# Sparse attention in head pairs with a turned value product, and key selection by counting bits over six row blocks at once

## The reference

```python
sc = jnp.where(pos[None, None, :] <= tb[None, :, None], sc, NEG)
_, idx = lax.top_k(sc, topk)              # topk = 256
dist = tb[None, :, None] - idx
o_a = sparse_attend(qa_blk, take_rows(k_a, idx), take_rows(v_a, idx), dist >= 0, dist, table_a)
...
s = jnp.einsum('bqgrd,bqkgd->bqgrk', qg, k_sel).astype(f32) * HEAD_DIM ** -0.5
s = jnp.where(valid[:, :, None, None, :], s + bias, NEG)
p = jax.nn.softmax(s, axis=-1).astype(v_sel.dtype)
o = jnp.einsum('bqgrk,bqkgd->bqgrd', p, v_sel)
```

## Time and profile before

| | us |
|---|---|
| three runs | 3072.55, 3091.87, 3098.43; median 3091.87 |
| the profiled execution | 3101.05, its span 3099.2 |
| mean granted clock of PE | 0.925 of 2.4 GHz |
| projection, first half with the indexer's scores | 0 to 236 |
| projection, second half | 236 to 517.8 |
| window attention | 517.8 to 643 |
| sparse attention, blocks 0 and 1 | 643 to 690 |
| sparse attention, blocks 2 and 3 | 690 to 757 |
| sparse attention, blocks 4 and 5 (to 852.8) | from 757 |
| sparse attention, blocks 6 and 7 | to 930 |
| sample attention | 930 to 1018 |
| merge | 1018 to 1077 |
| output projection, MLPs, recurrent mixer | 1077 to 3099 |

### The profile page before, as it was taken

How to read it: one execution, slowest core, us unless ns; L and a number is a source line. 1 busy time by engine, 2 the same in 40 slices (tenths; PEclk the granted TensorE clock), 3 DMA queues, 4 the chain that set the end, 5 groups by cost and what they waited for, 6 DMA issues and landing times. The chain is left out here.

```text
span 3099.2 us, 39640 instructions
## 1 busy us (share of the span) xinstructions
PE 2863.1 (92%) x15920; PEld 2603.2 (84%) x15920; DVE 1331.8 (43%) x2126; ACT 666.6 (22%) x1204; POOL 949.0 (31%) x488
## 2 busy tenths in 40 slices
PE   6789997779999389999999999899699999999999
PEld 6558777756774289999999999788689999999999
DVE  4158897786541443222222224465624222222222
ACT  4232222643342121100011002243411100011000
POOL 3014430002240253323333235323233333333332
PEclk8889998955598599999999999999899999999999
DMA  4212224312003411111111111213211111111112
GB/s 132 74 46 75 87 82 158 114 49 79 17 28 97 161 43 46 42 47 41 47 41 45 43 41 41 69 58 114 109 43 40 42 41 47 41 47 41 41 47 79
DMA packets 103765, 196.50 MB, mean 63 GB/s; under 512 B 24205, under 2 KB 58125, under 8 KB 103373
## 3 DMA queue, kind: packets, MB, share of 16 engines
q1 hardware_dynamic: 103650, 194.97, 19.6%
HBM read 169.92 MB, written 46.06 MB: 70 GB/s over the span
## 5 line engine op out<-in xcount | busy, mean ns | idle before, releaser
L1852 POOL TENSOR_TENSOR unit_low<-unit_raw,unit_high 128x1024 fp32r<-128x1024 f32 x160 | 450.1, 2814 | 1237.7 <-DVE unit_high L1848 1237.0
L2144 DVE TENSOR_TENSOR x_t<-x_t,m_ps 128x1092 f32<-128x1092 f32 x128 | 165.4, 1292 | 522.9 <-PE m_ps L1865 522.9
L1865 PE MATMUL m_ps<-m_hidden_high,unit_high 128*128 128x364 f32 x1536 | 341.5, 330 | 3.1 <-POOL m_hidden_low L2051 2.9
L1865 PE MATMUL m_ps<-xg_high,unit_high 128*128 128x364 f32 x1536 | 339.7, 329 | 0.0
L1865 PE MATMUL m_ps<-m_hidden_high,unit_low 128*128 128x364 f32 x1536 | 339.6, 329 | 0.0
L1865 PE MATMUL m_ps<-xg_low,unit_high 128*128 128x364 f32 x1536 | 338.8, 328 | 0.0
L1865 PE MATMUL m_ps<-m_hidden_low,unit_high 128*128 128x364 f32 x1536 | 338.4, 328 | 0.0
L1865 PE MATMUL m_ps<-xg_high,unit_low 128*128 128x364 f32 x1536 | 338.0, 328 | 0.0
L2132 DVE TENSOR_TENSOR m_relu<-m_relu,rstd_all 128x1092 f32<-128x1092 f32 x64 | 83.0, 1297 | 583.6 <-ACT m_relu L2078 583.6
L2078 ACT ACTIVATE m_relu<-m_ps 128x1092 f32<-128x1092 f32 x64 | 69.4, 1084 | 1210.5 <-PE m_ps L1865 1210.5
L1865 PEld LDWEIGHTS m_ps<-m_hidden_high,unit_high 128*128 128x128 f32 x1536 | 265.4, 188 | 12.0 <-POOL m_hidden_low L2051 7.9
(11 more groups left out here) (305 smaller groups left out, 4214.9 us busy)
## 6 DMA issues: line engine op xcount, KB each, us to landing
unit_raw<-w_units SPq DMA_DIRECT2D x160, 512.0 KB, 3.5
w_raw<-w_in SPq DMA_DIRECT2D x48, 256.0 KB, 2.9
proj_rows<-rows SPq DMA_DIRECT2D x32, 256.0 KB, 2.0
s_win<-win_cache SPq DMA_DIRECT2D x2, 3968.0 KB
sw_rows<-proj_rows SPq DMA_DIRECT2D x16, 384.0 KB, 3.7
proj_rows<-rows SPq DMA_DIRECT2D x36, 128.0 KB, 1.8
select_work<-xt SPq DMA_DIRECT2D x8, 546.0 KB, 3.8
x_t<-xt SPq DMA_DIRECT2D x4, 1092.0 KB, 11.9
```

What stands on the lines that cost most here:

```text
L1852: self.nc.gpsimd.tensor_tensor(self.wl[slot][:, :], self.raw[:, slot, :], self.wh[slot][:, :].bitcast(F32), ALU.subtract).then_inc(self.w_ ...
L1865: last = self.nc.tensor.matmul(ps[:, c, 0:CH], w[wslot][:, wk], v[:, k, c, :], start=(k == 0 and n == 0), stop=(k == nk - 1 and n == 2))
L2144: nc.vector.tensor_tensor(d.x[:, n, :, :], d.x[:, n, :, :], ps[s][:, :, 0:CH], ALU.add).then_inc(d.taken[s], 1)
```

## The change

**Selection.** A class `Select` finds, for every row, the 256th largest score bit by bit, for all six blocks at once. A step y from 0 to 31 counts for each block how many scores are at least a bound (a `tensor_scalar` with an accumulated sum, six of them) and then sets the next bit of the bound (one small instruction for y = 0, two for the others). The six steps that follow make the masks, one block each: count those above the bound, mark ties, count them along the row (`tensor_tensor_scan`), keep as many as there is room for, and write the mask. Steps 0 to 29 run in the projection, the eight others in the window stage, and none in the sparse stage.

```diff
+    def step(self, dve, y):
+
+        nc = self.nc
+        bound = self.bound[:, :].bitcast(F32)
+        if y <= BITS:
+            for x in range(NSEL):
+                v = self.scores(x)
+                dve.wait_ge(self.done, self.n)
+                nc.vector.tensor_scalar(self.junk[:, 0:v.shape[1]], v, bound[:, x:x + 1] if y else 0.0, 0.5 - TOPK, ALU.is_ge, ALU.add,
+                                        accum_out=self.count[:, x:x + 1]).then_inc(self.done, 1)
+                self.n += 1
+            dve.wait_ge(self.done, self.n)
+            said = self.count[:, :].bitcast(I32)
+            if y == 0:
+                self.mark(nc.vector.tensor_scalar(self.bound[:, :], said, 31, 1 << 30, ALU.arith_shift_right, ALU.bitwise_xor))
+            else:
+                b = BITS - y
+                self.mark(nc.vector.tensor_scalar(self.flip[:, :], said, 31, b, ALU.logical_shift_right, ALU.logical_shift_left))
+                dve.wait_ge(self.done, self.n)
+                self.mark(nc.vector.scalar_tensor_tensor(out=self.bound[:, :], in0=self.flip[:, :], scalar=1 << (b - 1) if b else 0,
+                                                         in1=self.bound[:, :], op0=ALU.bitwise_xor, op1=ALU.bitwise_xor))
+            return
+        x = y - BITS - 1
+        v = self.scores(x)
+        w = v.shape[1]
+        junk, tied, top = self.junk[:, 0:w], self.tied[:, 0:w], bound[:, x:x + 1]
+        dve.wait_ge(self.done, self.n)
+        self.mark(nc.vector.tensor_scalar(junk, v, top, None, ALU.is_gt, ALU.add, accum_out=self.count[:, x:x + 1]))
+        self.mark(nc.vector.tensor_scalar(tied, v, top, None, ALU.is_equal))
+        dve.wait_ge(self.done, self.n)
+        self.mark(nc.vector.tensor_scalar(self.room[:, x:x + 1], self.count[:, x:x + 1], -1.0, float(TOPK), ALU.mult, ALU.add))
+        self.mark(nc.vector.tensor_tensor_scan(junk, tied, tied, 0.0, ALU.add, ALU.max))
+        dve.wait_ge(self.done, self.n)
+        self.mark(nc.vector.scalar_tensor_tensor(out=tied, in0=junk, scalar=self.room[:, x:x + 1], in1=tied, op0=ALU.is_gt, op1=ALU.mult))
+        dve.wait_ge(self.done, self.n)
+        self.mark(nc.vector.scalar_tensor_tensor(out=junk, in0=v, scalar=top, in1=tied, op0=ALU.is_lt, op1=ALU.max))
+        dve.wait_ge(self.done, self.n)
+        nc.vector.tensor_scalar(v, junk, NEG, None, ALU.mult).then_inc(self.done, 1)
+        self.n += 1
+        dve.wait_ge(self.done, self.n)
+        nc.vector.memset(self.room[:, x:x + 1], 0.0).then_inc(self.ready, 1)
...
-                r1 = ROUNDS_1 * (n + 1) // len(steps)
-                for r in range(r0, r1):
-                    if ROUNDS[r][1] == 0:
-                        dve.wait_ge(S["masked"], SEL_TILES.index(ROUNDS[r][0]) + 1)
-                    topk_round(nc, link, work, m8, r)
+                r1 = SELECT_1 * (n + 1) // len(steps)
+                for y in range(r0, r1):
+                    if y == 0:
+                        dve.wait_ge(S["masked"], NSEL)
+                    sel.step(dve, y)
...
-                r1 = ROUNDS_1 + (ROUNDS_2 - ROUNDS_1) * (t + 1) // (NJ + 2)
-                for r in range(r0, r1):
-                    topk_round(nc, link, work, m8, r)
+                r1 = SELECT_1 + (sel.STEPS - SELECT_1) * (t + 1) // (NJ + 2)
+                for y in range(r0, r1):
+                    sel.step(dve, y)
```

```diff
-                nc.gpsimd.tensor_tensor(um[:, m % 2, 0:w], strip[:, h, P * (7 - j):SEQ],
-                                        work[:, WORK_OFF[j]:WORK_OFF[j] + w], ALU.add).then_inc(masked, 1)
+                    pool.wait_ge(maxed, 2 * SCORED[MASKED[m - 2] + 1])
+                if p == 0:
+                    pool.wait_ge(sel.ready, SEL_TILES.index(j) + 1)
+                keep = work[:, WORK_OFF[j]:WORK_OFF[j] + w].rearrange("p (o n) -> p o n", o=1).broadcast_to([P, 2, w])
+                nc.gpsimd.tensor_tensor(um[:, m % 2, :, 0:w], strip[:, p:AH:REP, P * (7 - j):SEQ], keep, ALU.add).then_inc(masked, 1)
...
+                if p == 0 and j >= 2:
+                    act.wait_ge(inverted, j - 1)
+                for e in range(2):
+                    nc.scalar.activation(s[:, t % 2, e, 0:w], s[:, t % 2, e, 0:w], ACT.Exp, bias=nm[:, t % 2, e:e + 1],
+                                         accum_out=ls[:, j % 2, 2 * p + e:2 * p + e + 1]).then_inc(exped, 1)
+
+            def take_probs(t):
+                if t >= 2:
+                    act.wait_ge(pv_done, t - 1)
+                for n, (e, k0, nk) in enumerate(turn_units(t)):
+                    if e == 0:
+                        act.wait_ge(probs_turned, TURNED[t] + n + 1)
+                        nc.scalar.activation(pt[:, t % 2, 0, P * k0:P * (k0 + nk)], pst[n % 2][:, 0:P * nk], ACT.Copy
+                                             ).then_inc(taken[0], 1)
...
                 if t >= 1:
-                    j, h = ITEMS[t - 1]
...
+                    take_probs(t - 1)
+                    if p == 1 and j < LAST_J:
                         take_turn(3 + j)
+                    if p == REP - 1:
+                        take_sums(j)
+                    if t >= 2 and ITEMS[t - 2][1] == REP - 1:
+                        take_spread(ITEMS[t - 2][0])
+            take_spread(LAST_J)
...
+                for n, (x, y) in enumerate(score_units(t)):
+                    u = SCORED[t] + n
+                    if u >= 2:
+                        pe.wait_ge(maxed, 2 * (u - 1))
+                    for e in range(2):
+                        b = HD * e
+                        last = nc.tensor.matmul(pss[u % 2][:, e, 0:y], qt[b:b + HD, j % 2, P * p:P * (p + 1)],
+                                                kt[b:b + HD, x:x + y], start=True, stop=True)
+                    last.then_inc(scored, 1)
...
+                for n, (e, k0, nk) in enumerate(turn_units(t)):
+                    pe.wait_ge(exped, 2 * t + e + 1)
+                    if n >= 2:
+                        pe.wait_ge(taken[0], TURNED[t] // 2 + n - 1)
+                    elif t:
+                        pe.wait_ge(taken[0], TURNED[t] // 2)
+                        pe.wait_ge(taken[1], TURNED[t] // 2 + n - 1 if len(turn_units(t - 1)) > 2 else TURNED[t] // 2)
+                    for k in range(nk):
+                        last = nc.tensor.transpose(pst[n % 2][:, P * k:P * (k + 1)],
+                                                   s[:, t % 2, e, P * (k0 + k):P * (k0 + k + 1)], ident[:, :])
                     last.then_inc(probs_turned, 1)
 
+            def turn_sums(j):
+                pe.wait_ge(turn_taken, min(4 + j, 3 + LAST_J))
+                if j == LAST_J:
+                    pe.wait_ge(spread_taken, j)
+                pe.wait_ge(inverted, j + 1)
+                nc.tensor.transpose(psx[0:AH, 0:P], li[:, j % 2, :], ident[:, :]).then_inc(sums_turned, 1)
...
+            def spread_sums(j):
+                if j == 0:
+                    pe.wait_ge(picked, 2)
+                pe.wait_ge(sums_taken, j + 1)
+                for p in range(REP):
+                    last = nc.tensor.matmul(psx[:, P * p:P * (p + 1)], pick[:, p, :], lt[:, j % 2, :], start=True, stop=True)
+                last.then_inc(spread, 1)
...
             def outputs(t):
-                j, h = ITEMS[t]
-                pe.wait_ge(probs_taken, UNITS[t + 1])
-                if h == 0 and j:
...
+                pe.wait_ge(taken[0], TURNED[t + 1] // 2)
+                pe.wait_ge(taken[1], TURNED[t + 1] // 2)
+                if p == 0 and j:
                     pe.wait_ge(normed, j)
-                g = h // REP
                 for k in range(j + 1):
-                    last = nc.tensor.matmul(pso[:, HD * h:HD * (h + 1)], pt[:, t % 2, P * k:P * (k + 1)],
-                                            v[:, k, HD * g:HD * (g + 1)], start=(k == 0), stop=(k == j))
+                    for e in range(2):
+                        last = nc.tensor.matmul(pso[HD * e:HD * (e + 1), P * p:P * (p + 1)], v[:, k, HD * e:HD * (e + 1)],
+                                                pt[:, t % 2, e, P * k:P * (k + 1)], start=(k == 0), stop=(k == j))
                 last.then_inc(pv_done, 1)
...
+                    dve.wait_ge(pv_done, t - 1)
+                for n, (e, k0, nk) in enumerate(turn_units(t)):
+                    if e == 1:
+                        dve.wait_ge(probs_turned, TURNED[t] + n + 1)
+                        nc.vector.tensor_copy(pt[:, t % 2, 1, P * k0:P * (k0 + nk)], pst[n % 2][:, 0:P * nk]).then_inc(taken[1], 1)
+
```

```diff
-                    if t >= 3:
-                        dve.wait_ge(probs_turned, UNITS[t - 2])
-                    if t >= 4:
-                        dve.wait_ge(negated, t - 3)
-                    nc.vector.tensor_tensor_reduce(out=s[:, t % 3, 0:w], in0=pss[t % 2][:, 0:w], in1=add, scale=1.0,
-                                                   scalar=NEG, op0=ALU.add, op1=ALU.max,
-                                                   accum_out=mx[:, t % 4:t % 4 + 1]).then_inc(maxed, 1)
```

(35 more changed lines are left out.)

248 lines of the change are left out of this document (129 added, 119 removed).

## The result

The changed kernel took 3109.54 us, median of 8 runs (3103.53 to 3110.89); the kernel before took 3095.05, median of 8 (3070.59 to 3101.83). The ratio is 1.0078, with a 95% interval of 1.0041 to 1.0115 (the two medians alone would give 1.0047), and every run of the changed kernel is longer than every run of the kernel before: slower by about 0.8%, where the prediction had 3025 and a range of 2985 to 3078. The runs of the kernel before lie in two groups, near 3071 with a mean granted clock of 0.930 to 0.936 and near 3100 with 0.924 to 0.926, and both of its profiled executions belong to the second.

The account below looks back on a forecast made before the run. PE was taken to bound the projection and the heavy sparse blocks (half of that the clock), short chains the window stage. Terms -3 - 6 - 59 + 1 = -67 gave 3034 profiled, 3025 us as median; range 2985 to 3078.

Parts of the forecast that it names:

- A: Projection: count steps of 6.0 us hidden behind PE, barrier 3.9 us earlier, blocks delaying norms; sum -3 us (-4 to +5).
- B: Window stage: DVE has 47 us of selection instead of 59.5, in eight blocks of 4 to 7.6; -6 us (-20 to +6).
- C: Sparse stage: paired heads overlap, PE waits for copies from block 4, clock mostly 2.4 GHz; 220 us against 279, -59 (-90 to +0).
- D: Merge and the rest: fewer transposes, but more instructions and smaller DMA pieces; +1 us (-2 to +4).
- 1: Sparse outputs: column halves don't overlap, 0.45 us per key block, whole 3058 us; chance 0.12.
- 2: Sparse stage: clock stays at 1.2 GHz throughout, 273 us instead of 220, whole 3078 us; chance 0.10.
- 3: Projection and window stage: counts with a sum run like the scan, 10.4 us a step, whole 3137 us; chance 0.04.
- 4: Better: sparse clock 1.00 nearly throughout (191 us), or counts at two elements per cycle with it; whole 2988 us; chance 0.13.

Follow-up runs that it names:

- run 1: Changed kernel with the selection's instructions handed out one by one, evenly over DVE's places in projection and window stage, instead of whole steps: 3059.86 us.
- run 10: Changed kernel with each selection step cut in two halves of about 3 us, spread over the same places: 3074.27 us.
- run 4: Changed kernel with selection handed out evenly, query loads issued one block earlier, and ACT's copies ahead of the next item's exponentials: 2961.91 us.
- run 3: Changed kernel with ACT's two copies of turned probabilities put ahead of the next item's negation and exponentials: 3013.67 us.
- run 7: run 4 with the output products of the two heads one head after the other instead of alternating: 2980.24 us.
- run 9: run 4 with the final selection steps of blocks 6 and 7 moved from the window stage to items 16 to 25 of the sparse stage: 2966.7 us.

## Why the prediction was wrong

The measured time lies outside the range of 2985 to 3078; a time within 1% of 3091.87, where it lies, had a chance of 0.19. Two steps failed, A's and B's price of a block of DVE work, and one term of C was mis-sized, the clock.

**A, failed in one step.** The step's length (6.3 for 6.0), the room on DVE and the earlier barrier (11.3 us to 7.2, 4.1 gained for 3.9 predicted) were right. Wrong was "the norm of a tile queues behind it, then ACT's root, POOL and the store: a loss of 0 to 8 us", of which the sum had about 1. That list ends with the store, for which nobody waits. It left out that the low parts of the weights stand on POOL behind the gains of the late tile, and PE waits for them. It cost 15.5 us; run 1 and run 10 give it back.

**B, failed.** "-6 (-20 to +6)" was +31. The blocks were named, but set off against 12 us saved, as if they cost only their excess at the end (+3). A job's chain goes twice through DVE (maxima, output copy), so a block of 6 us holds up the jobs in flight, and then DVE itself idles: it waits 49 us in all for outputs, where it waited 17 before. The clock follows (0.70 for 0.87). Served evenly the same work gives -3.6 (run 1), in pieces of 3 us +12.5 (run 10).

**C, right in its mechanism and wrong in its sizes.** Right were the overlap of the halves (in run 4, at full clock, one pair of outputs each 0.22 us, as predicted), the wait in 16 pairs (60.3 us, 4.3 at most; "about 4 us in each pair" was predicted), and nearly the period at 2.4 GHz: 147 us for the four blocks, with 154.7 measured at 0.98. The term that was mis-sized is the clock: "2.4 GHz for two thirds of blocks 4 to 7", 165 us, with 188.5 measured. The granted 0.76 is 2.4 GHz for half of the time, which by the prediction's 147 and 207 gives 176. The other 12 are the longer period and the place of the low clock, on the work behind each wait. The window stage, which I took for a pattern, keeps PE idle for a quarter of the time, behind its first loads in pieces of 3.8 us at most; here it idles for 4 us at a stretch. That the kernel before ran for 157 us at 1.2 GHz with PE always busy, and the new sparse stage in run 3 at 2.4, the prediction put down to the two row halves; no run tests this, and run 7 excludes only the overlap of the outputs. And "SP's query loads ... wait themselves for nothing that is late" was wrong by 7.9 us: I looked at what they wait for and not at what stands ahead of them. Blocks 0 to 3 without it take 51 us, for 55. The 279 us of the stage before are 276.5 by PE's records (650.2 to 926.7), so the same terms are worth 56 and not 59.

**D** was right (+0.4 for +1).

**The rivals.** 1 (no overlap) fell by the trace and run 7. 2 (clock at 1.2 GHz in the whole stage) didn't happen, but was nearer than the forecast in the heavy blocks (207, 188.5 measured, 165). 3 fell: a further element of a count takes 1.07 ns (0.60 us for 384, 1.28 for 1024), not 2.28. 4 fell too: the clock doesn't stay up, and a count of 1024 takes 1.28 us, where the mask's plain compare of the same row takes 0.75, so two elements per cycle is not had with an accumulated sum. That the Trainium skill has a change of the tiling mode drain TensorE (TensorEngine Tiling (Array Packing), "Key Properties") can be bounded for one such change: in run 4 eight turns ahead of outputs take 1.05 us (774.66 to 775.71) where the earlier trace rows has 0.93, so at most 0.12. The slower side had no rival with the right name; the blocks of DVE work should have been it.

## What to carry to other kernels

Fewer microseconds on an engine are worth nothing if they come in larger pieces: ask what stands behind the longest piece, on its engine and one engine further, and cut it down. In the projection pieces of 3 us were short enough (507 us, as with single instructions); in the window stage each cut paid (158, 139, 123). Price a wait on the matrix engine together with the clock that it costs, which was 34 us on top of 55. When a stage gets faster, look again at what is fetched for it, and at what is queued ahead of that.

## What the runs showed of the hardware

- A DVE instruction with two inputs in SBUF, or a plain `tensor_scalar`, gets longer by nearly the time that it stands beside a `tensor_tensor` of POOL: in run 9 a scan takes 5.31 us for 2.28 (3.17 beside POOL), a `tensor_scalar` 3.40 for 0.75 (2.86 beside it), a compare-and-combine of 1024 4.22 for 1.28 (3.14 beside it). The counts, with one input and a sum, don't: in run 4, 18 of the 32 counts of 1024 in the projection stand beside a busy POOL, and none takes more than 1.28 us. The Trainium skill says so (GPSIMD Engine Reference, "Specifications": contention with DVE instructions in a two-port mode or with two SBUF inputs), and these rows agree. An idle share of DVE is no room for such work where POOL is busy.
- PE's granted clock rose from 0.76 to 0.98 when transposes without use filled its waits of 4 us, and to 1.00 when they were short (9.1 us in all, run 3).
- An accumulated sum is read out by an instruction of its own, which takes 0.08 us after each count, with 0.04 us until the next count (in the changed kernel 319.96 to 320.04 and 320.08).
